# First SwiGLU of a one-core encoder layer: pairs 13 to 21 of the up projection as seven block products, its modulation dots moved

## The reference, cut to what matters

```python
x = _layernorm(x, ln_in_g, ln_in_b)
c_act = jax.nn.silu(c)
mod = (c_act @ w_ada[l] + b_ada[l]).reshape(B, N_SUBLAYERS, 3, D)
shift, scale, gate = mod[:, :, 0], mod[:, :, 1], mod[:, :, 2]

h = x * (1.0 + scale[:, 0, None, :]) + shift[:, 0, None, :]
y = _swiglu(h, ffn1_w_in[l], ffn1_w_out[l])        # silu(h @ Wg) * (h @ Wu), then @ w_out
x = _layernorm(ALPHA * x + 0.5 * gate[:, 0, None, :] * y, ...)
...                                                 # attention and pooling, with mod 1
h = x * (1.0 + scale[:, 2, None, :]) + shift[:, 2, None, :]
y = _swiglu(h, ffn2_w_in[l], ffn2_w_out[l])
x = _layernorm(ALPHA * x + 0.5 * gate[:, 2, None, :] * y, ...)
```

## Time and profile before

| | us |
|---|---|
| median of three runs | 937.65 (937.12 to 939.71) |
| the profiled execution | 938.05 |
| its span | 936.2 |
| PE busy in the span | 923.8 (99%) |
| DVE busy | 600.9 (64%) |
| ACT busy | 422.4 (45%) |
| POOL busy | 275.8 (29%) |

### The profile page before, as it was taken

How to read it: one execution, slowest core, us unless ns; L and a number is a source line. 1 busy time by engine, 2 the same in 40 slices (tenths; PEclk the granted TensorE clock), 3 DMA queues, 4 the chain that set the end, 5 groups by cost and what they waited for, 6 DMA issues and landing times.

```text
span 936.2 us, 12697 instructions
## 1 busy us (share of the span) xinstructions
PE 923.8 (99%) x4845; PEld 777.1 (83%) x4845; DVE 600.9 (64%) x875; ACT 422.4 (45%) x673; POOL 275.8 (29%) x239
## 2 busy tenths in 40 slices
PE   8999999999999999999999999999999999999997
PEld 5788888888888888787776677889999999888886
DVE  6956776445454964687775577788777777533334
ACT  6753223332322232483576646655556555322124
POOL 0021111111112522155863655832111111035124
PEclk9999999999999999999999999999999999999999
DMA  9936556656653663324421112196777775623402
GB/s 359 377 113 213 192 186 206 193 180 202 192 180 129 202 227 128 102 68 135 114 67 46 46 51 86 67 258 159 181 192 181 178 193 148 225 79 107 123 18 90
DMA packets 50507, 144.88 MB, mean 155 GB/s; under 512 B 5264, under 2 KB 7440, under 8 KB 50448
## 3 DMA queue, kind: packets, MB, share of 16 engines
q1 hardware_dynamic: 45008, 134.65, 43.0%
q0 software_dynamic: 4896, 8.92, 6.1%
q10 hardware_dynamic: 544, 0.52, 0.2%
HBM read 138.83 MB, written 4.19 MB: 153 GB/s over the span
## 4 chain that ended last, share of the span: by engine, by line
PE 95%; DMA 2%; DVE 1%; SPq 1%; ACT 1%; issue 0%; ACTq 0%; DVEq 0%
PE bank L890 23%; PE bank L892 23%; PE bank L891 23%; PE bank L1001 6%; PE bank L1003 6%; PE bank L1002 6%; PE bank L1304 2%; DMA raw<-wunits 1%; PE bank L1328 1%; DMA ada_first<-ada_w 1%; PE bank L1315 1%; PE bank L1068 1%; PE bank L975 1%; PE bank L976 1%; PE bank L969 0%
## 5 line engine op out<-in xcount | busy, mean ns | idle before, releaser
L1431 DVE TENSOR_TENSOR w_lo<-raw,w_hi 128x1024 fp32r<-128x1024 f32 (+1 forms) x117 | 160.7, 1383 | 132.1 <-ACT w_hi L1403 131.7
L890 PE MATMUL bank<-h_hi,w_hi 128*128 128x512 f32 x455 | 178.9, 393 | 0.0
L892 PE MATMUL bank<-h_hi,w_lo 128*128 128x512 f32 x455 | 177.4, 390 | 0.0
L891 PE MATMUL bank<-h_lo,w_hi 128*128 128x512 f32 x455 | 177.3, 390 | 0.0
L1403 ACT ACTIVATE w_hi<-raw 128x1024 fp32r<-128x1024 f32 (+1 forms) x118 | 118.7, 1023 | 116.5 <-PE bank L892 111.6
L890 PE MATMUL bank<-a_hi,w_hi 128*128 128x512 f32 (+1 forms) x338 | 128.3, 379 | 0.0
L891 PE MATMUL bank<-a_lo,w_hi 128*128 128x512 f32 (+1 forms) x338 | 127.9, 378 | 0.0
L892 PE MATMUL bank<-a_hi,w_lo 128*128 128x512 f32 (+1 forms) x338 | 127.8, 378 | 0.0
L2539 POOL TENSOR_TENSOR a_lo<-act_t,a_hi 128x512 fp32r<-128x512 f32 x27 | 37.7, 1395 | 251.5 <-ACT a_hi L1526 251.4
L892 PEld LDWEIGHTS bank<-h_hi,w_lo 128*128 128x128 f32 x455 | 85.5, 188 | 18.0
L890 PEld LDWEIGHTS bank<-h_hi,w_hi 128*128 128x128 f32 x455 | 85.5, 188 | 17.9 <-issue 0.5
(11 more groups left out here) (374 smaller groups left out, 1949.2 us busy)
## 6 DMA issues: line engine op xcount, KB each, us to landing
raw<-wunits SPq DMA_DIRECT2D x110, 512.0 KB, 3.5
ada_ring<-ada_w SPq DMA_DIRECT2D x56, 512.0 KB, 4.4
raw_ab<-wunits SPq DMA_DIRECT2D x18, 512.0 KB, 4.7
ada_first<-ada_w SPq DMA_DIRECT2D x16, 512.0 KB, 11.6
raw<-wunits SPq DMA_DIRECT2D x32, 256.0 KB, 3.8
raw<-wunits POOLq DMA_DIRECT2D x32, 256.0 KB, 4.8
raw<-wunits SPq DMA_DIRECT2D x16, 384.0 KB, 2.9
raw_d<-wunits SPq DMA_DIRECT2D x17, 256.0 KB, 2.7
```

The costliest lines, as they stand in the source:

```text
L890: mm(out, lh, rh, start=first, stop=False)
L891: mm(out, lh, rl, start=False, stop=False)
L892: return mm(out, ll, rh, start=False, stop=last)
L1431: nc.vector.tensor_tensor(lo, raw_of(n, width), hi.bitcast(F32), SUB).then_inc(s_lo, 1)
```

## The change

The first SwiGLU gets a block stage for pairs 13 to 21, written as the second one's: `block_products(f)`, `block_stage(base, f)` and the rest take the SwiGLU as an argument, with pair numbers t that count 22 more for the second. To make room, parts of the block stage lie on memory that others use: `t_hi1` lies on `x`, which is stored to DRAM in pair 5 and loaded back in the down projection; `raw_d41`, `lo_d41` and the copies lie on `c_act` and `ada_ring`, so no dot can run in pairs 11 to 21, and `c` is loaded and its silu taken a second time.

```diff
-ROPE_FIRST, ROPE_ACT = 4, 16
+ROPE_CHUNKS = {3: (0,), 4: (1,), 5: (2,), 6: (3,), 7: (4,), 8: (5,), 9: (6,), 10: (7, 8)}
...
+FIRST, END = (13, FT + 5), (FT, 2 * FT)
...
+DOTS_UP = [0] * EARLY + [1, 1] + [1, 2] * 6 + [1, 1]
+DOTS_DOWN = [0, 2, 2, 1, 1, 1] + [2, 3, 2] * 3 + [2, 2, 2]
```

`DOTS_UP` gives the dots of each half pair (22 in pairs 3 to 10), `DOTS_DOWN` those of each step of the down projection (34 in steps 1 to 17). SP's queue:

```diff
+            for i, tiles in enumerate(ADA_UP_STEPS):
+                n = split_next(F1, i)
+                if n is not None and n + RAWS < EDGE[0]:
+                    unit(n + RAWS)
+                for a in tiles:
+                    if a + 2 < ADA_UP:
+                        ada(a + 2)
+                if i == EARLY + 4:
+                    sp.wait_ge(*res_done(0))
+                    spill_x(0)
+            load_blocks(0)
+            sp.wait_ge(s_blk, PRODUCT["p3", END[0] - 1])
+            sp.dma_start(c_act[:], c_rows).then_inc(s_c, 16)
+            sp.wait_ge(s_bsum, SUM["gb", END[0] - 1])
+            ada(ADA_UP)
+            reload_x(0, 0)
+            ada(ADA_UP + 1)
+            for i in range(1, 4):
+                reload_x(0, i)
+            unit(F1_DOWN + LEAD + 2)
+            for i, tiles in enumerate(ADA_STEPS):
+                unit(F1_DOWN + LEAD + 3 + i)
+                for a in tiles:
+                    if a + 2 < RING_TILES:
+                        ada(a + 2)
```

DVE in the up and down projection (`ffn`), and ACT's additions:

```diff
-                for t in range(early, FT + 1 if f == 0 else T0 - 1):
+                whole = local(FIRST[f])
+                for t in range(early, whole - 1):
                     for j in range(2):
...
+                        for a in ADA_UP_STEPS[2 * t + j] if f == 0 and 2 * t + j < len(ADA_UP_STEPS) else ():
+                            ada_ring_tile(a)
                         if j == 0 and t >= early + 1:
                             product(base, f, t - 1)
+                    for c in ROPE_CHUNKS.get(t, ()) if f == 0 else ():
+                        rope_chunk(c)
+                combine_h(f)
+                for j in range(2):
+                    rest(*combo_key(f, j))
+                product(base, f, whole - 2)
+                block_stage(base, f)
                 if f == 0:
-                    dve.wait_ge(s_adadone, ADA_FIRST + UP - EARLY)
+                    dve.wait_ge(s_adadone, ADA_FIRST + ADA_UP)
                     derive_gate(0)
-                    derive_in(1)
-                    derive_gb(1)
-                    derive_gate(1)
...
                         if n < STREAM:
                             dve_lo(dve, n)
-                        a = UP - EARLY + DPM * m + j
-                        if f == 0 and a < RING_TILES:
+                        i = DPM * m + j
+                        for a in ADA_STEPS[i] if f == 0 and i < len(ADA_STEPS) else ():
+                            if a == ADA_UP:
+                                dve.wait_ge(s_cact, 3)
                             ada_ring_tile(a)
+                        if f == 0 and i == 1:
+                            dve.wait_ge(s_adadone, ADA_FIRST + 3 * KD)
+                            derive_in(1)
+                            derive_gb(1)
...
+                    if f == 0 and 3 <= t < 3 + KD:
+                        k = t - 3
+                        fn(h_full[0][:, k, :], x[:, k, :], ACT.Identity, scale=first_col[:, k, 0:1],
+                           bias=first_col[:, k, 1:2]).then_inc(s_hf[0], 1)
...
+                        if f == 0 and m == 0 and j == 1:
+                            act.wait_ge(s_c, 32)
+                            fn(c_act[:], c_act[:], ACT.Silu).then_inc(s_cact, 1)
```

More of the change, by code:

```diff
@@ L95, in product_order @@
     out = []
[L96 to L104, removed]
+    for first, end in zip(FIRST, END):
+        for t in range(first, end + 1):
+            if t < end:
+                out += [("p1", t), ("p5", t), ("p6", t)]
+            if t > first:
+                out.append(("p4", t - 1))
+            if t < end:
+                out += [("p7", t), ("p2", t)]
+            if t > first:
+                out.append(("p3", t - 1))
@@ L105, in product_order @@
     return out
 def rounding_order():
[L110 to L115, removed]
+    out = []
+    for f, (first, end) in enumerate(zip(FIRST, END)):
+        out += [("T", 4 * f + j) for j in range(4)] + [("ab", first), ("13", first), ("2", first)]
+        for t in range(first, end + 1):
+            if t > first:
+                out.append(("d4", t - 1))
+            if t + 1 < end:
+                out += [("ab", t + 1), ("2", t + 1), ("13", t + 1)]
@@ L116, in rounding_order @@
     return out
 def rest_order():
[L121 to L126, removed]
+    out = []
+    for f, (first, end) in enumerate(zip(FIRST, END)):
+        out += [("T", 4 * f), ("T", 4 * f + 1), ("ab", first), ("13", first), ("2", first),
+                ("T", 4 * f + 2), ("T", 4 * f + 3)]
+        for t in range(first, end + 1):
+            if t > first:
+                out.append(("d4", t - 1))
+            if t + 1 < end:
+                out += [("ab", t + 1), ("2", t + 1), ("13", t + 1)]
@@ L127, in rest_order @@
     return out
 def sum_order():
[L132 to L141, removed]
+    out = []
+    for f, (first, end) in enumerate(zip(FIRST, END)):
+        out += [("T", 4 * f + j) for j in range(4)] + [("s2", first), ("s4", first)]
+        for t in range(first, end + 2):
+            if t - 2 >= first:
+                out.append(("gb", t - 2))
+            if first <= t - 1 < end:
+                out.append(("ga", t - 1))
+            if t + 1 < end:
+                out += [("s2", t + 1), ("s4", t + 1)]
+            if first <= t - 1 < end:
+                out += [("ub", t - 1), ("pa", t - 1)]
@@ L147, in silu_order, with combo_key @@
     out = []
[L148 to L152, removed]
+    for first, end in zip(FIRST, END):
+        for t in range(first, end + 2):
+            if t - 2 >= first:
+                out.append(("b", t - 2))
+            if first <= t - 1 < end:
+                out.append(("a", t - 1))
     return out
 def copy_order():
[L158 removed]
+    return [(kind, t) for first, end in zip(FIRST, END) for t in range(first, end) for kind in ("p1", "u2", "u3")]
+def combo_key(f, j):
+    return "T", 4 * f + j
 def counts(order, base):
@@ L1638, in up @@
             def up(base, f):
-                for t in range(FT + 1 if f == 0 else T0 - 1):
-                    if t < FT and split_next(base, 2 * t) is not None and (f == 0 or t >= 2):
+                whole = local(FIRST[f])
+                for t in range(whole - 1):
+                    if split_next(base, 2 * t) is not None and (f == 0 or t >= 2):
                         act_hi(act, split_next(base, 2 * t))
@@ new lines, in a_low, with block_stage @@
+                dve.wait_ge(s_ah[f], m + 1)
+                dve.wait_ge(s_al[f], m)
+                hi, lo = a_parts(f, m)
+                tt(lo, act_t[:, t % 2, :], hi.bitcast(F32), SUB).then_inc(s_al[f], 1)
+            def block_stage(base, f):
+                first, end = FIRST[f], END[f]
+                weight_sums(first)
+                rest("ab", first)
+                rest("13", first)
+                rest("2", first)
+                product(base, f, local(first) - 1)
+                rest(*combo_key(f, 2))
+                rest(*combo_key(f, 3))
+                for t in range(first, end + 1):
+                    if t >= first + 2:
```

620 lines of the change are left out of this document (337 added, 283 removed).

## The result

The changed kernel takes **964.59 us** (median of four runs, 962.97 to 965.77), the kernel before 938.0 beside it: the ratio is 1.028 (95% interval 1.027 to 1.030), 26.6 us slower. The forecast was 958 with a range of 946 to 965, slower. The profiled execution took 965.07 us, its span 963.1 us, 26.9 more than before.

A forecast was written before the change was run, and what follows sets the result against it. PE was taken as the bound, busy 99% of the span, so time is the columns it streams. 938.05 - 6.2 (nine block pairs) + 26.5 (stalls behind moved dots) = 958.4 us, median 958, range 946 to 965.

The forecast's parts named there:

- the large term: Tiles 1 to 5 of the first SwiGLU's down projection: moved dots make DVE late, stalling PE by 26.5 us.
- seven dots: Down projection, DVE's time from one residual to the next with seven dots: 22.3 us, against PE's 14.96; with six, 17.9.
- DVE's delay at residual 5: Down projection: DVE's summed lateness there, 31.2 us against a PE that never waits.
- the four megabytes at the start of the stage: Loads queued at the down projection's beginning: DVE put 2.5 us late at residual 1 (0 to 5).
- Nine pairs: Pairs 13 to 21 of the first SwiGLU as block products: 7.2 us saved, net -6.2 us.
- The start of the stage: First block pair: 1.0 us lost, taken from the second SwiGLU, most of it the wait for ACT's copy.
- Pairs 3 to 10: First SwiGLU before the blocks, with more dots and the 2 MB store: PE loses 0, up to 3 us.
- B: Rival: the cover holds in the down projection, delay never passes what PE can bear; 931.9 us, chance 0.08.
- C: Rival: ring refills come sooner in the down projection, turn 4.2 us, stalls 13.2 us; 945 us, chance 0.09.
- D: Rival: longer loss from pair 5's store, DVE 5 us late at the down projection, or turn 5.97; 966 us, chance 0.06.
- E: Rival: first SwiGLU's blocks miss 10.08 us a pair; up to 3 us more, counted within the forecast case's 0.77.
- the 946.6 us: Whole-kernel time by the skill's DMA estimate of 3.2 us per 512 KB: buffer turn 4.35, stalls 14.7 us.

The follow-up runs named there:

- ACT's new order: Changed kernel with ACT's rounding of the last pair's product moved behind this pair's silu and second weight rounding in pairs 3 to 11; alone 960.21 us (1.025).
- fastest version: Changed kernel with four dot buffers in the down projection, ACT's rounding moved later in pairs 3 to 11, dots spread with few behind tile 1; 933.1 us (0.995).
- the run with the late store: Changed kernel with the 2 MB store of x issued five steps later on SP, in pair 7 to 8 instead of pair 5; 966.16 us (1.030).

## Why the prediction was right, and by how much it was off

The profiled execution was forecast at 958.4 us and took 965.07. The three terms below missed by 2.4, 0.55 and 3.8 us, all to the slow side, and make up the 6.7. The way and the cause of the large term were worked out; that the time still fell inside the range was narrow, 0.4 us.

- **What bounds, and the large term: right.** Stalls of PE behind DVE's `w_lo`, before units 11, 14, 17, 20 and 21, as worked out. Forecast 26.5 us, measured 28.9. The parts: seven dots 22.0 and 22.8 us (forecast 22.3), six 18.8 (17.9), DVE's delay at residual 5 31.1 us (31.2; residual 5 starts at 385.79, where PE without a wait would end the tile at 294.82 + 4 x 14.96 = 354.7). That the last is met so closely is luck, as two errors cancel: the four megabytes at the start of the stage made DVE 0.5 us late at residual 1 (it begins on that tile at 295.29), not 2.5, and the tiles from residual 1 to 5 took 2.0 us more than forecast. Unit 21 came 27.2 us late (26.5), and 1.7 us of a low clock behind its stall were the rest.
- **Nine pairs: right in kind, 0.55 us short.** -5.65 for -6.2. The start of the stage cost 1.55 us where the second SwiGLU's 1.0 was taken: two more waits of 0.2 us for a rest stood beside the 0.5 us for the copy.
- **Pairs 3 to 10: the step that failed.** It was put at 0, "up to 3 us if that lead is gone", and cost 3.8: nearly 2 us in the wait before the first block product, the rest in the pairs before it. The busy time of 9.0 of 10.88 us was taken as the measure of DVE's slack, but DVE and ACT wait for each other once in a pair, 2.13 us of it, so there was hardly any slack to win back what was lost around the 2 MB store. A lead of three units is spent once; what matters is how fast it is refilled. In four other kernels with this very up stage the first block product lay at 170.3, 170.8, 171.4 and 172.4 us, so the loss scatters from 1.8 to 3.9 us; in the four later ones with ACT's new order it lay at 167.9 to 169.2.
- **Rivals.** B and C are out by the stalls. The time falls in D's strip, over 963, which had 0.06: its store in pair 5 has its part in the 3.8 us, but its late start of 5 us and its mean turn of 5.97 us did not occur (the means of the tiles from residuals 2, 3 and 4 are 5.46, 5.72 and 5.93 us; of all eight turns, 5.7, where the forecast had 5.53). E cost 0.5 us.
- **The Trainium skill.** By the rule of the Trainium skill ("DMA: Bandwidth & Descriptors", Anatomy of one DMA) a load of 512 KB is an estimate of 3.2 us; but that section fits DMAs that GpSimd issues, and the ring's are issued by SP. The quickest of the ring's landed in 3.4 us in this trace, the median in 4.5, so the 946.6 us from it was out by 18. By the Trainium skill ("TensorE: Matmul & The Clock Gate", Part 1) an idle PE is put back to 1.2 GHz; here the trace agrees. Behind the stall before unit 11 the timeline of PE shows it:

```profile
326.74 0.80 PE L1022 MATMUL bank<-a_hi,w_hi 128*128 128x512 f32 x1 [5.92 <-DVE w_lo L1565]
327.34 0.63 PE L1023 MATMUL bank<-a_lo,w_hi 128*128 128x512 f32 x1
327.76 0.63 PE L1024 MATMUL bank<-a_hi,w_lo 128*128 128x512 f32 x1
...
332.02 0.39 PE L1022 MATMUL bank<-a_hi,w_hi 128*128 128x512 f32 x1
```

The step is 0.42 to 0.43 us from matmul to matmul (327.76 - 327.34) up to 332.02, then 0.23. The granted clock from 327.8 to 332.0 is 0.50, the level of 1.2 GHz.

- **Left open.** Whether the blocks would keep their 5.65 us with more dots beside them wasn't tried. A wait of 0.8 to 1.4 us for ACT's copy came in single block pairs of some runs and not in others. In the one that was followed back it stood behind a late load of `raw_d`; why that load was late is not known. How much of the fastest version's 4.5 us the reordering of ACT brings with other dots was not separated, and the dots behind tile 1 were not varied alone with four buffers.

## What to carry to other kernels

Before work with its own transfers is moved into a shorter stretch, compute the period of its buffers there: here the period of a tile on the in-order DVE was the fixed work in front, plus what lies before the first dot on the buffer that ends last, plus that buffer's turns, plus one dot, and the busy share told nothing of it. Look for a buffer that lies idle in that stage: with the work spread evenly the stage was 15.6, 3.8 and 0.1 us longer than before with two, three and four buffers. Neither step did it alone here (four buffers with the dots unspread left 7.0 us). The turn must be measured anew with each number of buffers, as in most tiles it came out longer than the 5.5 us carried over. Look in the same way for a loop between two engines when a lead is to pay for a one-time delay: without slack in the loop the lead is never refilled.

## What the runs showed of the hardware

- The landing of a 512 KB load grew from 4.3 to 5.1 and 5.6 us (medians) when two, three and four buffers were in use for the same loads; the stage was then 149, 131 and 127 us long.
- While POOL's tensor operations ran, DVE's operations on 1024 columns took 2.1 to 2.3 us in place of 1.2.
- After an idle stretch of PE of 2.9 us (the run with the late store) the granted clock was 0.50 and a matmul step 0.43 us for 6 us; after the 5.92 us stall, for 5.3 us. Behind a wait of 1.9 us before unit 21 the clock was 0.50 in the changed kernel (397 to 400 us) and 1.00 in the run with ACT's order (393 to 396 us).
